# Leaving the 16 meta tokens' columns out of the blocks whose results for them are not read

## What is computed

```python
xp = concatenate([meta_tokens, x_prompt])               # 16 + 512
h = rmsnorm(x); z, xbc, dt, sc_b, sc_c, sc_h, g_ssd, g_sc = split(h @ w_in)
xbc = silu(causal_dwconv(xbc, conv_hist, conv_w) + b)   # 4 taps, along time
xs, Bm, Cm = split(xbc)
for each chunk:                                         # state runs over ALL tokens
    y = diag(Cm, Bm, decay, dt, xs) + Cm @ h_prev * exp(acum)
    h_prev = chunk_decay * h_prev + Bm * to_end @ xs
u = grouped_rmsnorm((y + D*xs) * silu(z));  y_ssd = u @ w_ssd_out
y_sc = (sc_b * causal_dwconv(sc_c * sc_h)) @ w_sc_out   # 3 taps
x = x + (sigmoid(g_ssd) * y_ssd + sigmoid(g_sc) * y_sc) @ w_o
x = x + experts(rmsnorm(x))                             # top-2 of 8, in the top-1 group of 4
y_prompt = final_rmsnorm(xp)[:, N_META:]
```

## Time and profile before

| | us |
|---|---|
| median of 3 runs | 1317.38 |
| lowest, highest | 1317.21, 1318.74 |
| span of the profiled execution (first to last instruction) | 1316.0 |
| PE busy in it | 1201.4 |
| DMA, mean over the span | 160 GB/s |

### The profile page before, as it was taken

The page is one execution under the profiler, slowest core; times in us unless marked ns, Lnnn a source line. Parts: engine busy times, 40 slices in busy tenths (PEclk is TensorE's granted clock), DMA queues, the critical chain, the costliest instruction groups (busy, mean ns, idle before and its releaser), DMA issues.

```text
span 1316.0 us, 22259 instructions
## 1 busy us (share of the span) xinstructions
PE 1201.4 (91%) x8729; PEld 1033.6 (79%) x8729; DVE 531.9 (40%) x839; ACT 386.9 (29%) x568; POOL 458.6 (35%) x358
## 2 busy tenths in 40 slices
PE   5999999999999999999999999999996979777781
PEld 5999999999986986897698689999995646443340
DVE  5445432002556765685576551014444241121112
ACT  4221114433524433442443352122324001010112
POOL 5444432333543453363345443434320111111200
PEclk8999999998999999999999999999998989999996
DMA  6333322232411620541251132343639999999985
GB/s 157 80 82 80 80 64 65 65 94 62 132 49 59 159 64 16 158 106 33 82 151 50 32 105 81 85 129 107 210 113 347 408 399 397 403 398 396 415 331 161
DMA packets 185566, 210.67 MB, mean 160 GB/s; under 512 B 12166, under 2 KB 161798, under 8 KB 176754
## 3 DMA queue, kind: packets, MB, share of 16 engines
q1 hardware_dynamic: 176626, 193.41, 44.1%
q0 software_dynamic: 5040, 9.72, 3.0%
q10 hardware_dynamic: 3822, 6.39, 1.3%
HBM read 191.56 MB, written 26.57 MB: 166 GB/s over the span
## 4 chain that ended last, share of the span: by engine, by line
PE 73%; DMA 10%; DVE 6%; SPq 5%; issue 3%; ACT 2%; POOL 1%; ACTq 0%; DVEq 0%; POOLq 0%
PE acc L641 47%; SPq L562 5%; PE pTS L1031 4%; PE acc L920 4%; DMA big<-in_w_up 4%; PE acc L1072 2%; DMA ring<-in_w_gate 2%; DMA area<-in_w_up 2%; DVE area L1235 2%; PE pTS L820 2%; PE pY L814 1%; PE pY L838 1%; PE acc L779 1%; PE pO L768 1%; DVE area L1233 1%
## 5 line engine op out<-in xcount | busy, mean ns | idle before, releaser
L641 PE MATMUL acc<-h_parts,ring_parts 128*128 128x328 f32 (+1 forms) x3840 | 548.2, 304 | 6.3 <-DVE area L1280 2.2
L641 PEld LDWEIGHTS acc<-h_parts,ring_parts 128*128 128x128 f32 x3840 | 534.3, 191 | 21.3 <-issue 15.3
L1894 POOL TENSOR_TENSOR ring_parts<-ring,ring_parts 128x1024 fp32r<-128x1024 f32 x112 | 280.5, 2505 | 435.3 <-ACT ring_parts L1602 435.2
L1602 ACT ACTIVATE ring_parts<-ring 128x1024 fp32r<-128x1024 f32 x112 | 118.4, 1058 | 392.5 <-PE acc L641 367.2
L1031 PE MATMUL pTS<-area,big 128*64 128x256 f32 x672 | 105.7, 395 | 18.2 <-DMA area<-in_w_gate 5.4
L641 PE MATMUL acc<-u_parts,ring_parts 128*128 128x264 f32 (+1 forms) x640 | 109.4, 299 | 0.0
L1031 PEld LDWEIGHTS pTS<-area,big 128*64 128x64 f32 x672 | 65.2, 143 | 49.8 <-DMA area<-in_w_gate 8.9
L641 PEld LDWEIGHTS acc<-u_parts,ring_parts 128*128 128x128 f32 x640 | 96.4, 188 | 0.0
L641 PE MATMUL acc<-area_parts,ring_parts 128*128 128x264 f32 (+1 forms) x512 | 91.1, 299 | 0.0
L1235 DVE SCALAR_TENSOR_TENSOR area<-area,xvec 128x616 f32<-128x616 f32 x72 | 84.9, 1179 | 10.5 <-DVE area L1233 0.6
L641 PEld LDWEIGHTS acc<-area_parts,ring_parts 128*128 128x128 f32 x512 | 78.4, 188 | 0.0
(11 more groups left out here) (353 smaller groups left out, 1437.9 us busy)
## 6 DMA issues: line engine op xcount, KB each, us to landing
ring<-in_w_in SPq DMA_DIRECT2D x80, 512.0 KB, 4.0
area<-in_w_gate SPq DMA_DIRECT2D x21, 1024.0 KB, 25.4
area<-in_w_up SPq DMA_DIRECT2D x21, 1024.0 KB
area<-in_w_down SPq DMA_DIRECT2D x21, 1024.0 KB, 23.7
area<-in_state_ssm SPq DMA_DIRECT2D x16, 512.0 KB, 6.9
out<-area SPq DMA_DIRECT2D x16, 512.0 KB, 5.5
ring<-in_w_ssd_out SPq DMA_DIRECT2D x16, 512.0 KB, 4.0
ring<-in_w_gate SPq DMA_DIRECT2D x7, 1024.0 KB, 17.4
```

Of the source, the lines that this page charges most:

```text
L641: m = nc.tensor.matmul(acc[a][:, h, 0:n], w[s][:, k, :], x[:, k, h * HALF:h * HALF + n], start=first and k == 0 and w is w_hi and x is hi, ...
L1602: a_.activation(w_hi[b % 2], w_raw[b % 2], ACT.Copy).then_inc(hi_done, 1)
L1894: gp.tensor_tensor(w_lo[b % 2], w_raw[b % 2], w_hi[b % 2].bitcast(F32), ALU.subtract).then_inc(lo_done, 1)
```

## The change

Columns 0 to 15 (`LIVE` = 16) are left out of each block of which nothing reads them. In blocks whose columns 12 to 15 are still read by a convolution, columns from 12 on are kept (`CONV_FROM`). The blocks' columns become:

- s blocks: from 12 (two of three, 580 columns: 258 + 322) or from 16 (the third, 576: 256 + 320).
- o1, z, gate and mix blocks: from 16 (256 + 320). wo blocks: from 16, as 288 + 288.
- in a group b 0 (C): from 12. B and the four x tiles (b 1 to 5): all 592, as before.

DVE and ACT work on these blocks is shortened by the same columns. The convolution of b 0 and its SiLU start at 16, and so do the three taps of the short convolution. The scan itself, dt, B, x, the state and the normalisation of u stay at 592 (two memsets on POOL set the unwritten parts of C and of z to 0; two other memsets go). From the wo blocks on there are 576 tokens in tiles of 128, 128, 128, 128 and 64 (before, the last had 80), so `h2_rows`, `y_sum`, the router and the expert lists hold 576 rows. The prompt's rows now start on a tile, so loads and stores that were cut in two are one.

```diff
+LIVE = N_META
+KEPT = T - LIVE
+CONV_FROM = N_META - 4
+KROWS = [P] * 4 + [KEPT - 4 * P]
-ROUNDS = -(-(T - CAP) // LATER)
+ROUNDS = -(-(KEPT - CAP) // LATER)
-DUMP, NO_TOKEN = T, 2048
+DUMP, NO_TOKEN = KEPT, 2048
...
+        def s_first(b):
+            return LIVE if b % 3 == 2 else CONV_FROM
+
+        def g_first(turn, b):
+            if b >= 10:
+                return LIVE if turn == GROUPS - 1 else g_first(turn + 1, b - 10)
+            return CONV_FROM if b == 0 else LIVE if b >= 6 else 0
...
-        def pe_block(pe, where, b, hi, lo, first=True, last=True, part=None):
+        def pe_block(pe, where, b, hi, lo, at, first=True, last=True, part=None):
...
+            mid = (at + TP) // 2
             for k in range(8):
                 for w, x in ((w_hi, hi), (w_hi, lo), (w_lo, hi)):
                     for h in (range(2) if part is None else (part,)):
-                        n = HALF if h == 0 else T - HALF
-                        m = nc.tensor.matmul(acc[a][:, h, 0:n], w[s][:, k, :], x[:, k, h * HALF:h * HALF + n],
+                        c = slice(at, mid) if h == 0 else slice(mid, T)
+                        m = nc.tensor.matmul(acc[a][:, h, 0:c.stop - c.start], w[s][:, k, :], x[:, k, c],
...
-                        for h, n in ((0, HALF), (1, T - HALF)):
-                            m = nc.tensor.matmul(acc[a][:, h, 0:n], w[f % 2][:, k, :], x[:, k, h * HALF:h * HALF + n],
+                        n = KEPT // 2
+                        for h in range(2):
+                            m = nc.tensor.matmul(acc[a][:, h, 0:n], w[f % 2][:, k, :], x[:, k, LIVE + h * n:LIVE + (h + 1) * n],
...
-                    sp.dma_start(xr[0:N_META, 0, :], meta).then_inc(x_again, 16)
-                    sp.dma_start(xr[N_META:P, 0, :], xp[0:P - N_META, :]).then_inc(x_again, 16)
-                if 4 <= f < 7:
-                    sp.dma_start(xr[:, f - 3, :], xp[(f - 3) * P - N_META:(f - 2) * P - N_META, :]).then_inc(x_again, 16)
+                if 3 <= f < 7:
+                    sp.dma_start(xr[:, f - 3, :], xp[kept(f - 3), :]).then_inc(x_again, 16)
...
-                    link(v.tensor_scalar(o_, raw[:, c % 2, 0:XCONV], w[:, 0, 0:1], None, ALU.mult))
+                    at = LIVE if c == 0 else 0
+                    o_ = cv[:, c % 2, at:XCONV]
+                    link(v.tensor_scalar(o_, raw[:, c % 2, at:XCONV], w[:, 0, 0:1], None, ALU.mult))
...
-            link(gp.memset(s_pad[:, 0, 0:SH], 0.0))
-            link(gp.memset(s_pad[:, 1, 0:SH], 0.0))
...
+            gp.memset(cT[:, 0:LIVE], 0.0)
+            link(gp.memset(sz[:, :, 0:LIVE], 0.0))
```

More of the change, by code:

```diff
@@ L889, in row_sums @@
                 for i in range(TILES)[::-1]:
-                    m = nc.tensor.matmul(pY[0:ROWS[i], 180 + i:181 + i], x[:, tok(i)], ones[:, 0:1], start=False, stop=last and i == 0)
+                    m = nc.tensor.matmul(pY[0:KROWS[i], 180 + i:181 + i], x[:, kept(i)], ones[:, 0:1], start=False, stop=last and i == 0)
                 return m
@@ L968, in _ @@
             nc.tensor.matmul(pY[:, 192:192 + NE], ones[:, :], before[:, TILES - 2, :], start=True, stop=False)
-            nc.tensor.matmul(pY[:, 192:192 + NE], ones[0:R4, :], mm[0:R4, TILES - 1, :], start=False, stop=True).then_inc(r_pos, 1)
+            nc.tensor.matmul(pY[:, 192:192 + NE], ones[0:TS, :], mm[0:TS, TILES - 1, :], start=False, stop=True).then_inc(r_pos, 1)
             def to_rows(u, s):
@@ L1078, in _ @@
             pe.sem_inc(m_end, 1)
-            n_most = pe.value_load(most[0:1, 0:1], min_val=0, max_val=T)
+            n_most = pe.value_load(most[0:1, 0:1], min_val=0, max_val=KEPT)
             with pe.If(n_most > CAP):
@@ L1359, in _ @@
                 dve.wait_ge(x_c, f + 1)
-                for h, n in ((0, HALF), (1, T - HALF)):
-                    row = x2T[:, f, h * HALF:h * HALF + n]
+                n = KEPT // 2
+                for h in range(2):
+                    row = x2T[:, f, h * n:(h + 1) * n]
                     x = v.tensor_tensor(row, row, acc[a][:, h, 0:n], ALU.add)
@@ L1536, in _ @@
             dve.wait_ge(m_end, 1)
-            n_most = dve.value_load(most[0:1, 0:1], min_val=0, max_val=T)
+            n_most = dve.value_load(most[0:1, 0:1], min_val=0, max_val=KEPT)
             with dve.If(n_most > CAP):
@@ L1635, in gate_of @@
                 act.wait_ge(o_m, read)
-                a0, a1 = acc_parts(acc[a])
-                g0, g1 = halves(to)
+                a0, a1 = acc_parts(acc[a], LIVE)
+                g0, g1 = halves(to, LIVE)
                 a_.activation(g0, a0, ACT.Sigmoid)
@@ L1676, in silu @@
                     bias = xvec[:, bass.ds(conv_tile(g, c), 1), 4:5].rearrange("p a b -> p (a b)")
-                    v0, v1_ = conv_parts(cv[:, c % 2, :], XH, XROW)
-                    d0, d1 = halves(dst)
+                    at = LIVE if c == 0 else 0
+                    v0, v1_ = conv_parts(cv[:, c % 2, :], XH, XROW, at)
+                    d0, d1 = halves(dst, at)
                     a_.activation(d0, v0, ACT.Silu, bias=bias)
@@ L1782, in _ @@
                 act.wait_ge(w_x, f + 1)
-                a_.activation(ssum if f == 0 else sqb[:, f % 2, :], x2T[:, f, :], ACT.Square).then_inc(q_sq, 1)
+                a_.activation((ssum if f == 0 else sqb[:, f % 2, :])[:, 0:KEPT], x2T[:, f, 0:KEPT], ACT.Square).then_inc(q_sq, 1)
             act.wait_ge(r_lg, 1)
@@ L2072, in _ @@
             pool.wait_ge(m_end, 1)
[L2073 removed]
+            n_most = pool.value_load(most[0:1, 0:1], min_val=0, max_val=KEPT)
             with pool.If(n_most > CAP):
```

189 lines of the change are left out of this document (93 added, 96 removed).

## The result

The changed kernel takes 1302.37 us (median; 1301.62 to 1303.69), the kernel before 1317.47 us in the same comparison (1317.21 to 1318.74): 15.1 us less, ratio 0.9899 with a 95% interval of 0.9876 to 0.9922. The forecast was 1302.5 us. The profiled executions span 1316.0 and 1301.3 us, 14.7 us apart.

A forecast was written before the change was run, and what follows sets the result against it. The prediction took PE's columns to bound the dense blocks and transfers the expert stage. Columns 13.8, expert transfers 0.9 and final read and store 0.2 us sum to 14.9, so 1317.4 becomes 1302.5 us; bounds 1301.7 to 1304.6, range 1299.5 to 1308.

The forecast's parts named there:

- What bounds the kernel: PE bounds the s, gate, mix and wo blocks, transfers the expert stage; all 13.8 us pass on to its start.
- 0.45 ns a column: Flat price per removed PE column, from shapes of 264 and 328 columns; ends 0.417 and 0.462 ns.
- s blocks, 3.33 us: Gain in the s blocks from 7392 column passes, after a DVE wait in the first two blocks takes back 288.
- o1 blocks, 2.76 us: Gain in the o1 blocks: 6144 column passes at the flat price, PE running through them without waits.
- C, z and last group, 2.5 us: Gains in the groups: C blocks 0.52 us, z halves inside the scan 1.73 us, last group's gate blocks 0.26 us.
- Gate and mix, 3.80 us: Gain in gate blocks 2 to 7 and 16 mix blocks: 8448 column passes in the stretch without a gap.
- wo, 1.38 us, and the 64-row tile, nothing: wo blocks gain 1.38 us from 3072 column passes; the shorter last tile brings nothing, bounds 0 and 0.1 us.
- Transfers, 0.9 and 0.2 us: Fewer rows moved save 0.9 us in the expert stage (0 to 1.4) and 0.2 us in final read and store.
- Rival A: Weight load sets a floor at 121 ns, so first halves outside wo gain nothing: 1308.7 us, chance 0.07.
- Rival B: Half-clock stretches among dense blocks, one or two more or fewer, 1.7 us each: 1299.1 or 1305.9 us, chance 0.14.
- C: Granted clock falls to half at both ends of each of the four scans, costing 27 us: 1330 us, chance 0.02.
- D: Columns of z and C, or the transfers, bring nothing to the end: 1305.0 or 1303.6 us, chance 0.08.

The follow-up runs named there:

- e8: The changed kernel unaltered, run again on one chip beside its variants: 1303.39 us, ratio 0.9910 to the kernel before.
- e10: Changed kernel, second matmul of blocks cut at 12 reading 322 columns from 268 instead of 270, last two columns left out: 1299.90 us, one run.
- e1: Changed kernel with the last token tile carried with 80 rows again through wo and the router: 1299.29 us, ratio 0.9887.
- e5: Changed kernel with every block split at column 272, so second halves always have 320 columns: 1300.93 us, ratio 0.9900.
- e6: Changed kernel with every block split at column 272 and the last token tile of 80 rows: 1298.30 us, ratio 0.9877.
- e11: Changed kernel with first halves of blocks cut at 16 reading 240 columns instead of 256: 1295.95 us, one run.
- e4: Changed kernel, blocks cut at 16: the third product of each weight step takes 224 first-half columns instead of 256: 1302.71 us.
- e9: Changed kernel, second matmul of blocks cut at 12 reading 320 columns instead of 322, still from 270: 1303.15 us, one run.
- e3: Changed kernel with the blocks cut at 12 not cut at all, taking all 592 columns: 1304.65 us, ratio 0.9925.
- e7: Changed kernel with the 20 blocks cut at 12 cut at 8 instead, 260 + 324 columns: 1302.06 us, one run.

## Why the prediction was right, and where it wasn't

- **What bounds the kernel.** Right. PE's columns set the end from the s blocks through the mix blocks, and every gain there passed on to the expert stage: it starts 14.0 us earlier (1018.10, now 1004.08) and ends 14.5 us earlier.
- **0.45 ns a column.** Right as a mean, wrong as a price, and a mean that came out right by luck, since two of its parts (the level, and 258 + 322 from 270) were not in the sum. The step that failed is the line through the two shapes of one block, 264 and 328. It says what a long half costs more than a short one, and not what two or eight columns less of each will bring. Measured: 0.18 ns a column in the blocks cut at 12, 0.49 (high level) or 0.66 (low level) in those cut at 16.
- **s blocks, 3.33 us.** 22 of them gave 2.7 us instead of 3.2, for this reason (14 x 0.053 + 8 x 0.253 = 2.8). The first two and their surroundings gave 1.5 instead of 0.1. 0.7 us of it is the landing of `in_ln_w`, 4.81 us after its start instead of 5.49; in e8 it took 5.49 again, and the run of the 22 began at 37.87 us, 0.6 ahead of before. The rest is the two blocks themselves, 15.2 us from their first matmul instead of 16.0, and nearly all of it is the clock, as these stretches before and after show (the granted clock is the third number from the end):

```profile
22.45:38.45 16.00, 15.90 (x96) 15.63 (x96) 4.48 (x2) 1.73 (x4) 9.15 (x8) 0.82 0.26 66
...
21.77:36.97 15.20, 15.03 (x97) 14.77 (x97) 4.51 (x3) 1.80 (x4) 8.90 (x6) 0.86 0.27 69
```

16.0 x 0.82 and 15.2 x 0.86 are both 13.1 us at full clock. So the 1.5 us were no gain of the columns. The prediction placed the 2.1 us wait for DVE behind the first halves of these blocks. It stands ahead of both blocks' matmuls on PE (`h_parts` L1141), so it takes nothing back.
- **o1 blocks, 2.76 us.** Mis-sized: 3.8 us, or 0.61 ns a column. 12 of the 16 blocks ran at the low level: 4 x 0.187 + 12 x 0.253 = 3.8. All at the high level they would have given 3.0.
- **C, z and last group, 2.5 us.** Right: 2.6 us between the first scan and the mix blocks, and the wait at the first transposes grew by 0.30 us instead of 0.26.
- **Gate and mix, 3.80 us.** Right: 4.1 us, 22 x 0.187 at the high level. At the low one, as in e10, it would have been 5.5.
- **wo, 1.38 us, and the 64-row tile, nothing.** The first term was right by e1 (1.7 us); the second is the largest error. "Nothing (0 to 0.1)" measured 4.0 us in the wo stage, 2.6 us of the whole time between e5 and e6. The step argued from ten products of one tile size, 0.10 us each whatever their columns. No row of those read showed a tile of 64 rows between tiles of 128, and the bound against a loss was put at zero without a reason. Into a tile of 80 rows the step is as long as between full ones (108 and 111 ns), into one of 64 it is not.
- **Transfers, 0.9 and 0.2 us.** 0.5 and 0.2 us. Queue 0 moved 9.46 MB, as worked out.
- **Rival A**, the floor, falls for 256 columns: the pair fell from 272.8 ns to 265.0 or 262.2, and with first halves held at their old spacing it could have lost only the 3.6 ns of the longer ones. Something like it shows below 256: in e11 a part of what the first half saves is paid back by the matmul behind it, and in e4 half of it or all, by the level it is laid beside. The rule of the Trainium skill, "TensorE: Matmul & The Clock Gate", section "LDWEIGHTS (loading the stationary operand)", gives 107 ns for 128 columns; from it the prediction worked out that a cut below 256 columns would bring nothing. These runs agree with it in part: 240 columns in the shorter half brought less than the same cut in the longer one, but they did bring 3.3 or 6.1 ns a pair, and 224 columns were spaced at 103 ns, under the 107. So the load is no hard floor for one matmul here.
- **Rival B**, the clock's phase, happened, in the kernel's favour: one half-clock stretch of 3.4 us less, 1.7 us, and 0.8 us in the first two blocks. Together it covers more than half of the 4.0 us that the 64-row tile took. Behind the wo blocks a stretch of 3.4 us that was not there before (978.5 to 981.9 us) stands in the row that lost 0.2 us. (The prediction gave B's faster end as 1299.1 us and began its range at 1299.5.) **C** did not happen: no granted clock below 0.9 in the scans. **D** did not: the columns of z and C came through.

## What to carry to other kernels

When columns are cut from matmuls, take them from the longer of two halves that share a weight step, where the same 16 columns gave 2.8 ns a pair more than in the shorter one, and look at odd splits (258 + 322 columns from 270 were dearer than 260 + 324). Don't shorten a tile's rows from 80 to 64 among tiles of 128 without a look at the weight loads around it. And where a sum comes out right, check its terms by stage: here an error of 3.5 us and errors of 3.9 us had cancelled. Before a difference of a microsecond or two is put down to an edit, look at a stage that the edit leaves alone: here such stages moved by 1.3 to 1.5 us from run to run.

## What the runs showed of the hardware that was not expected

- A tile of 64 rows or columns between tiles of 128 made the steps into and out of it 203, 203, 210 and 156 ns long, against 108, 75, 111 and 71 ns with 80. The weights were not loaded ahead there.
- The spacing of one matmul can fall by far more than the cycle: 118 to 103 ns for 224 columns, and 145 or 147 to 156 ns for the one behind it (e4).
- 256 + 320 columns took either 262.2 or 265.0 ns a pair (6.293 or 6.360 us a block), over whole runs of blocks, at full granted clock. The 22 gate and mix blocks took 141.70 us in the kernel after, 141.69 in e9, and 140.25 in e10, whose program is the same there. It is worth 1.4 us, about as much as a single half-clock stretch. In the third s blocks, where no half-clock stretch lies, the level went by the blocks beside them: low in the kernel after, e1, e3 and e8, high in e5, e6, e7, e9 and e10. What sets it is open.

```profile
765.25 140.25 PE acc L655 x1056
```
